# Three rearrangements ahead of the expert stage of a fused decoder layer: one column and the taps in `prepare`, the step tables of the recurrence, and double-buffered sums instead of in-place ones for the shared expert

## What is computed

```python
z = x @ w_in
# group A: GLU, causal depthwise convolution of width 31, LayerNorm, swish
u = z_conv[..., :D_CONV] * sigmoid(z_conv[..., D_CONV:])
c = silu(layer_norm(conv(u_full, conv_w) + conv_b))
# group B: RWKV-7, 8 heads of 64; per token
s = s * w_t + (s @ a_t) b_t^T + v_t k_t^T ;  y_t = s r_t
o_rw = (group_norm(y) * gn_g + gn_b + bonus) * g
x = layer_norm(ALPHA * x + concat(c, o_rw) @ w_out)
# 64 experts, top 8 of each token, hidden width 256, and one shared expert
f = (silu(x @ sh_gate) * (x @ sh_up)) @ sh_down + routed experts
x = layer_norm(ALPHA * x + f)
```

## Time and profile before

| | us |
|---|---|
| median of 3 runs | 1219.98 |
| lowest and highest | 1216.82, 1224.33 |
| the profiled execution | 1224.33 |
| its span, first to last instruction | 1222.5 |
| PE busy in the span | 1093.1 |
| DVE, ACT, POOL busy | 540.6, 278.2, 191.6 |
| mean granted clock of PE, of 2.4 GHz | 0.95 |

### The profile page before, as it was taken

The page is one execution under the profiler, slowest core; times in us unless marked ns, Lnnn a source line. Parts: engine busy times, 40 slices in busy tenths (PEclk is TensorE's granted clock), DMA queues, the critical chain, the costliest instruction groups (busy, mean ns, idle before and its releaser), DMA issues. The chain is left out here.

```text
span 1222.5 us, 33491 instructions
## 1 busy us (share of the span) xinstructions
PE 1093.1 (89%) x14966; PEld 826.4 (68%) x14967; DVE 540.6 (44%) x1216; ACT 278.2 (23%) x583; POOL 191.6 (16%) x202
## 2 busy tenths in 40 slices
PE   6999997888799997999999999999899999999940
PEld 5887886767553584877777777777667676766720
DVE  0778968597475786342222222222222222222105
ACT  2146421122364120111111111111111111111102
POOL 2000100000000011122222212222222122221113
PEclk8999998888799999899999999999999999999975
DMA  7221131400532178999999999999999999999623
GB/s 201 69 53 52 52 88 24 108 7 5 185 105 56 71 276 357 375 342 347 343 341 336 333 327 328 322 321 327 331 331 321 336 338 329 344 330 334 229 34 140
DMA packets 87589, 279.58 MB, mean 229 GB/s; under 512 B 22363, under 2 KB 46948, under 8 KB 62605
## 3 DMA queue, kind: packets, MB, share of 16 engines
q1 hardware_dynamic: 72165, 240.07, 55.0%
q0 software_dynamic: 14336, 34.11, 11.6%
q10 hardware_dynamic: 944, 3.24, 0.7%
HBM read 258.80 MB, written 35.30 MB: 241 GB/s over the span
## 5 line engine op out<-in xcount | busy, mean ns | idle before, releaser
L2141 PE MATMUL pgu<-x_list_t,w_exp 128*64 128x96 f32 x8192 | 361.4, 248 | 23.5 <-DMA w_exp<-in_exp_up_dram 17.2
L2141 PEld LDWEIGHTS pgu<-x_list_t,w_exp 128*64 128x64 f32 x8192 | 344.1, 139 | 32.8 <-DMA w_exp<-in_exp_up_dram 21.6
L2168 PE MATMUL pyl<-w_exp,hid 128*96 128x512 f32 x512 | 230.5, 593 | 3.7 <-issue 2.3
L2195 POOL DMA_INDIRECT scr_f<-y_list,row x64 | 92.1, 1439 | 510.1 <-DVE row L890 159.2
L2156 DVE TENSOR_TENSOR sig<-sig,pgu 128x192 f32<-128x192 f32 x64 | 22.7, 354 | 312.3 <-ACT sig L2149 312.3
L507 PE MATMUL pz<-w_exp 128*128 128x260 f32 x672 | 160.4, 398 | 0.3 <-ACT w_exp L324 0.3
L2168 PEld LDWEIGHTS pyl<-w_exp,hid 128*96 128x96 f32 x512 | 80.1, 166 | 107.4 <-issue 104.1
L507 PEld LDWEIGHTS pz<-w_exp 128*128 128x128 f32 x672 | 131.1, 198 | 24.3 <-issue 3.0
L2186 DVE TENSOR_SCALAR y_list<-pyl,weight 96x512 f32<-96x512 f32 x64 | 47.8, 747 | 188.9 <-PE pyl L2168 149.6
L2149 ACT ACTIVATE sig<-pgu 128x192 f32<-128x192 f32 x64 | 21.2, 331 | 422.7 <-PE pgu L2141 422.7
L162 DVE SCALAR_TENSOR_TENSOR w_exp<-arena,w_exp 128x512 f32<-128x512 f32 x120 | 89.9, 750 | 3.8
(11 more groups left out here) (352 smaller groups left out, 1015.0 us busy)
## 6 DMA issues: line engine op xcount, KB each, us to landing
w_exp<-in_exp_gate_dram SPq DMA_DIRECT2D x64, 1024.0 KB, 38.6
w_exp<-in_exp_up_dram SPq DMA_DIRECT2D x64, 1024.0 KB, 38.8
w_exp<-in_exp_down_dram SPq DMA_DIRECT2D x64, 1024.0 KB, 38.7
w_exp<-in_w_in_dram SPq DMA_DIRECT2D x22, 512.0 KB, 3.9
w_exp<-in_x_prompt_dram SPq DMA_DIRECT2D x8, 512.0 KB, 5.4
w_exp<-in_w_out_dram SPq DMA_DIRECT2D x2, 2048.0 KB, 11.7
scr_x<-arena SPq DMA_DIRECT2D x4, 512.0 KB
scr_f<-arena ACTq DMA_DIRECT2D x4, 512.0 KB, 11.9
```

Source lines behind the costliest of these rows:

```text
L2141: last = nc.tensor.matmul(pgu[64 * half:64 * half + 64, s % 2, (2 * part + j) * CAP:(2 * part + j + 1) * CAP], w[job.slot][:, k, f0:P * ha ...
L2168: last = nc.tensor.matmul(pyl[0:CAP, c, :], hid[:, s % 2, j, :], m.expert_down[job.slot][:, j, c * 512:(c + 1) * 512], start=(j == 0), sto ...
L2195: nc.gpsimd.indirect_dma_start(m.scr_f, bass.IndirectOffsetOnAxis(ap=row[:, job.l:job.l + 1], axis=0), y_list[:, s % 2, :], None, bounds_c ...
```

## The change

Three parts. **A**, in `prepare`: on PE the last GLU column stands directly behind `turn_samples(0)` and the groups of `read_inside` follow one by one between the sample transposes; on DVE the taps are spread among the masks, seven in place of six, and `glu(3)` stands behind all of them but `mask_inside(7)`'s. **B**, in the recurrence: the group norm of tile 0 is inverted, normalised, finished and turned one step earlier, its bonus one step later; `finish_out(1)` moves from behind the loop into step 15, and `turn_out(1)` from the middle of the first mixing product to ahead of `outputs(3)`. **C**, the shared expert: the sum of tile i is written to `f0[:, i % 2]`, two buffers of 1024 columns in `x_area`, and stored from there; `residual(i)` for i of 2 and 3 waits for the store of tile i - 2, ACT's copy of the samples for that of tile 2. The wait for `x1_stored` ahead of `residual(0)` is gone, and so are the waits for the five stores in `experts`; SP waits for them at the end of `recur_and_mix`.

```diff
@@ prepare, PE
                 turn_samples(0)
+                col(cv + 5)
                 read_inside(4)
-                col(cv + 5, lambda: read_inside(5))
                 turn_samples(2)
+                read_inside(5)
+                turn_samples(4)
                 read_inside(6)
-                turn_samples(4)
                 read_inside(7)
@@ prepare, DVE
                 mask_inside(3)
+                taps.take(1)
                 mask_inside(4)
-                taps.take(5)
+                taps.take(2)
                 mask_inside(5)
+                taps.take(2)
                 mask_inside(6)
+                taps.take(2)
                 glu(3)
-                taps.take(1)
                 mask_inside(7)
@@ recur_and_mix, tables
-    INVERT = {10: 0, 13: 1}
-    NORMALISE = {11: 0, 14: 1}
-    FINISH = {12: 0}
-    TURN = {13: 0}
-    SCALE = {9: 0, 13: 1, 14: 2, 15: 3}
+    INVERT = {9: 0, 13: 1}
+    NORMALISE = {10: 0, 14: 1}
+    FINISH = {11: 0, 15: 1}
+    TURN = {12: 0}
+    SCALE = {10: 0, 13: 1, 14: 2, 15: 3}
@@ recur_and_mix, SP, at its end
+                sp.wait_ge(f_stored[0], 16 * 3)
+                sp.wait_ge(f_stored[1], 16 * 2)
@@ recur_and_mix, PE, behind the recurrence
+                turn_out(1)
                 outputs(TM - 1)
                 pe.wait_ge(spent_cleared, 1)
-                mix_part(0, 0, lambda: turn_out(1))
+                mix_part(0, 0)
@@ recur_and_mix, ACT
-                    act.dma_start(m.scr_f[t0:t0 + n, :], x1[0:n, i, :]).then_inc(m.f_stored[i], 16)
+                    act.dma_start(m.scr_f[t0:t0 + n, :], f0[0:n, i % 2, :]).then_inc(f_stored[i % 2], 16)
                 act.wait_ge(f_done, NT)
+                act.wait_ge(f_stored[TM % 2], 16 * (TM // 2))
@@ recur_and_mix, DVE
-                finish_out(1)
...
-                        if i == 0:
-                            dve.wait_ge(x1_stored, 16 * (NT + 2))
+                        if i >= 2:
+                            dve.wait_ge(f_stored[i % 2], 16 * (i // 2))
...
-                        nc.vector.scalar_tensor_tensor(x1[0:n, i, cs], x1[0:n, i, cs], ALPHA, out,
+                        nc.vector.scalar_tensor_tensor(f0[0:n, i % 2, cs], x1[0:n, i, cs], ALPHA, out,
@@ experts, DVE, ACT and POOL, each
-                for i in range(NT):
-                    dve.wait_ge(m.f_stored[i], 16)
```

More of the change, by code:

```diff
@@ L1035, in recur_and_mix @@
         hit_b = halfs[:, 2 * P:2 * P + NT * E].rearrange("p (i e) -> p i e", i=NT)
-        f_sample = m.x_area[0:B, 2 * D:3 * D]
+        f0 = m.x_area[:, 2 * D:4 * D].rearrange("p (b d) -> p b d", b=2)
         cnt = m.cnt
@@ L1110, in recur_and_mix @@
         f_taken = sem("f_taken")
-        m.f_stored = [sem(f"f_stored{i}") for i in range(NT)]
+        f_stored = [sem(f"f_stored{i}") for i in range(2)]
         late = COLS[NCOL - LATE:]
@@ L1782, in _ @@
                 act.wait_ge(f_done, NT)
+                act.wait_ge(f_stored[TM % 2], 16 * (TM // 2))
                 for c in range(4):
-                    last = nc.scalar.copy(f_sample[:, QD * c:QD * (c + 1)], quarter(ph[:, TM % 2, :], c))
+                    last = nc.scalar.copy(f0[0:B, TM % 2, QD * c:QD * (c + 1)], quarter(ph[:, TM % 2, :], c))
                 last.then_inc(sample_moved, 1)
@@ L2062, in residual @@
                         cs = slice(c * 512, (c + 1) * 512)
-                        out = ph[0:n, i % 2, cs] if i < TM else f_sample[:, cs]
-                        nc.vector.scalar_tensor_tensor(x1[0:n, i, cs], x1[0:n, i, cs], ALPHA, out,
+                        out = ph[0:n, i % 2, cs] if i < TM else f0[0:n, i % 2, cs]
+                        nc.vector.scalar_tensor_tensor(f0[0:n, i % 2, cs], x1[0:n, i, cs], ALPHA, out,
                                                        ALU.mult, ALU.add).then_inc(f_taken, 1)
@@ L2269, in _ @@
                 gate_act(act, Job(0))
-                for i in range(NT):
-                    act.wait_ge(m.f_stored[i], 16)
                 for q in range(E):
@@ L2282, in _ @@
                     gather(nc, m, pool, Job(q))
-                for i in range(NT):
-                    pool.wait_ge(m.f_stored[i], 16)
                 for q in range(E):
```

## The result

| | before | after |
|---|---|---|
| median, us | 1219.14 (20 runs) | 1226.61 (20 runs) |
| lowest and highest | 1215.63, 1225.44 | 1221.95, 1231.08 |
| span of the profiled execution | 1222.5 | 1229.0 |
| PE busy | 1093.1 | 1090.0 |

The ratio of the times is 1.0059, 95% interval 1.0044 to 1.0076: +7.2 us, where the forecast was +8.3 and 1228.0. The two profiled spans differ by 6.5 us.

What follows compares the result with a forecast made beforehand. The weight stream was taken as the expert stage's bound, with 35 us of PE slack. +7.3 (C) - 1.3 (A) + 2.3 (B) = +8.3 us: 1224.3 to 1232.6 profiled, 1228 on the 1219.98 median; range 1213 to 1239.

Steps and rivals of the forecast that it cites:

- The bound: Expert stage: the weight stream, 11.4 us a job against PE's 10.1, is the bound; PE has 35 us of slack.
- the dry point: Turn into the expert stage: weights queue empty at 505.1, 5.7 us after the next load's issue; a later start is free until then.
- Part C: Shared expert's residual: store waits start PE 15.6 us later, job 6's up weights land +7.3 us later; bounds 0 and 15.6.
- Store 2: Store of tile 2's sum: issued after residual 2 ends at 484.1, lands 11.9 us later, at 496.0.
- The fifth store: The samples' 32 KB store at the block's end: issued 498.9, landing after 2.1 us in a nearly quiet queue, at 501.
- PE's first row: Start of the expert block: PE begins at about 503.5, 15.6 us later than before.
- The landing into the dry queue: Job 6's up weights: landing 6.9 us after issue in an idle queue, at 522.3 against 514.9.
- Part A: End of prepare: SP's tail comes earlier and DVE's masks end with it; -1.3 us, bounds -2.5 to +1.5.
- Part B: Recurrence: step 9's later add less PE's idle +1.4, moved finish_out(1) and turn_out(1) +0.9; +2.3 us, bounds -6 to +6.
- Nothing absorbed: Turn into the expert stage: the whole 15.6 us delay passes, +16.6 in all, 1237 us; chance 0.22.
- Quick stores: Shared expert: stores take 4.7 us, residuals don't wait, block ends 3 us later; with recurrence at -6, 1213 us; chance 0.12.
- The recurrence at its bad end: Recurrence: both PE idle times return after the wait, +6 there, +12 in all, 1232 us; chance 0.11.

Runs made afterwards that it cites:

- the seven executions: Two of the changed kernel, plus C alone, both holds and both waits of C apart: last up weights 0.3 to 7.9 us later than before.
- C alone: The kernel before with only part C of the change: 1.0037 of before, +4.5 us.
- the changed kernel with the store moved up: Changed kernel, SP's store of the sample states behind one expert's loads instead of two, two more experts' loads before its wait: 1.0028 of before.
- the tables alone: Kernel before with only part B's step tables (tile 0's group norm a step earlier, bonus later); finish_out(1) and turn_out(1) unmoved: 0.9992 of before.
- both holds: Kernel before with six or eighteen unread ACT copies behind the last store issue of recur_and_mix: 0.9988 and 1.0029 of before.
- both waits of C apart: Kernel before with part C but its stores awaited inside experts, not by SP (1.0010); or in-place sums with SP's end-of-block wait replacing those in experts (1.0007).
- B alone: The kernel before with only part B of the change: 1.0003 of before.

## Why the prediction was right, by its steps

**The bound** held. PE waits for up weights at the end and the stream's pitch is 11.4 us a job (649.6 / 57). The sign and the size of the loss come from the lead at the turn. I had put the dry point at 5.7 us behind the next issue and took 8.3 off the delay (15.6 to 7.3), since a load into an idle queue lands sooner; the seven executions put the lead at 6.5. The 5.7 came out near it partly by luck: it read the end of the queue from the landing of job 5's down weights, and behind them the engines still have the `ln2` loads and gathers to carry.

**Part C**, forecast +7.3. The changed kernel's first expert load came 1.04 us earlier than before, so forecasts are to be read 1.04 lower. Residuals 2 and 3 then were due at 481.8 and 486.3 and came at 481.59 and 486.54. From there the steps miss in both directions:
- Store 2 was taken at 11.9 us; ACT's copy was due at 495.0 and came at 491.52. I had taken over the length of stores that stand behind one another in ACT's own queue. In the kernel before, counted in order, the first packet of store 2 starts 6.3 us behind its issue, when those of stores 0 and 1 are through; in the changed kernel nothing stands ahead of stores 2 and 3, their first packets start after 3.9 and 3.5 us, and store 3 landed after 7.8 us.
- The fifth store, 32 KB, was taken at 2.1 us from a quiet queue. From its issue to SP's next block are 5.1 us, against 0.8 where SP doesn't wait for it. Its first data packet starts 3.3 us and its last packet 4.1 us behind its issue, beside the weights of job 5, in flight until 500.8; the row from a quiet queue was the wrong one.
- PE's first row: due 502.5, came 499.64, 12.8 us late (from the first load, 63.69 against 50.92) and not 15.6. (The terms as written add up to 501 + 1.9 = 502.9 for the 503.5 of the forecast, so 0.6 of it is a slip.)
- The landing into the dry queue: 6.9 forecast, 8.7 measured; the first gate/up 7.89 instead of 7.49. A gather of POOL, issued at 514.14, runs beside this load and none ran beside the one of the 6.9. That is a likely reason, and no run tests it.

Up weights of job 6 were due at 521.3 and landed at 520.6. From the first load the loss is 84.65 - 78.0 = 6.7 us there, and 7.9 by the last issue. The runs by time say +4.5 (2.4 to 6.6) for C alone. The term is right in its mechanism, and its size is right in part by luck: a delay too long by 2.8 and a landing too short by 1.8 nearly cancel.

The rule of the Trainium skill (DMA: Bandwidth & Descriptors, "Queues, rings and completion order") by which a DMA engine serves its rings in turn gave about 0 for this term. I read the 10.2 and 11.9 us as speaking against the rule, and that reading was wrong. The packets of the changed kernel from 482.5 to 483.3 us, by queue (q1 is SP's, q10 ACT's, q0 POOL's; number of packets, MB, share of the engines):

```profile
q1 hardware_dynamic: 23, 0.16, 49.8%
q10 hardware_dynamic: 25, 0.10, 33.2%
q0 software_dynamic: 25, 0.06, 20.2%
```

The three queues have equal turns, as the rule says; in the kernel before SP's and ACT's have 111 packets each from 479.0 to 482.5. A store is slow all the same, and the packets show where its time goes. The first packet of tile 0's store starts 3.6 us behind its issue in the kernel before. Its packets are 4 KB and the weights' are 8 KB, and POOL's gathers take a turn too, so that its data takes another 4.6 us; 2.0 us later it is landed, 10.2 in all. The 3 to 4 us ahead of the first packet seem to belong to the traffic: with nothing ahead in ACT's own queue they are 3.3 to 4.0 us beside full engines, and at most 0.8 us for the one store that was issued as the share sank to 0.58 (the 32 KB one of the changed kernel with the store moved up, at 491.69). No run was made to test that.

**Part A**, forecast -1.3. SP's last loads begin at 228.07, against 230.63:

```profile
229.57 0.56 DVE L734 TENSOR_TENSOR w_exp<-pt,w_exp 128x384 f32<-128x384 f32 x1
...
231.04 0.27 DVE L1897 MEMSET x_area<- 128x256 f32 x1 [0.92 <-PEq L268]
...
228.07 1.34 SPq L311 DMA_DIRECT2D arena<-scr_sample  x2
...
229.45 1.02 SPq L312 DMA_DIRECT2D arena<-scr_sample  x1
```

The last mask of DVE (229.57 + 0.56) and SP's last load (229.45 + 1.02) now end within 0.4 us, as forecast. But of the 2.16 us by which the next block starts earlier (231.04 against 233.20), 1.45 were there before A's place (DVE's last solving reduction starts at 211.11 against 212.56). From that reduction to the add of the first step are on average 41.4 us in five executions with A (40.95 to 41.66) and 41.7 in nine without (40.58 to 42.47). A is worth -0.3 us with a scatter of half a microsecond; this term was over-read by one microsecond, inside its bounds.

**Part B**, forecast +2.3. In the changed kernel, against the earlier trace rows:

```profile
307.68 0.20 DVE L1827 RECIPROCAL arena<-arena 128x8 f32<-128x8 f32 x1 [8.78 <-ACT arena L1663]
...
311.63 0.42 DVE L1940 TENSOR_TENSOR x_area<-x_area,pst 128x256 f32<-128x256 f32 x1
...
323.54 0.69 DVE L1839 TENSOR_TENSOR w_exp<-w_exp 128x512 f32<-128x512 f32 x1 [7.38 <-ACT w_exp L1657]
...
325.80 6.35 PE L1407 MATMUL ph<-w_exp,arena 128*128 128x260 f32 x16
...
347.50 0.34 PE L1359 MATMUL pt<-x_area,w_exp 64*32 64x64 f32 x16
```

- The reciprocal of step 9 waits 8.78 us for ACT, and the add comes at 311.63 against 309.12, 3.8 us later measured from step 8's add (297.57 and 298.84). The forecast was 4.1.
- PE's gaps without a releaser, 2.5 and 2.7 us before, are gone or small:

```profile
PE pst L1346 <- issue: 0.5, 1, 0.5
```

  That was taken as a chance. In the six executions with B or its tables PE's matmuls have 0.5 to 3.4 us of such gaps from 300 to 350 us (1.9 on average), in the eight without 4.4 to 7.2 (6.0).
- The packets show what these gaps wait for. All 22 gaps of more than 1 us there, over the fourteen executions, end 1.25 to 1.60 us after a 16 KB transfer of the kind `instruction` has ended. In the kernel before such transfers end at 307.0, 312.85 and 319.05, and PE goes on at 308.46, 314.13 and 320.41. At an instant taken at random between 300 and 350 us such a transfer has ended 1.25 to 1.60 us ago in 6% of the cases. So these gaps are waits for PE's own next instructions. That they shrink with B because PE stands 8 us for DVE meanwhile fits, and no run separates it.
- Not foreseen: `SCALE` moved to step 10, so DVE's third operation of `finish_out(0)` waits 7.38 us for ACT's bonus, at 323.54 above. It does not lengthen the stretch: from step 8's add to step 12's are 37.5 us before and 37.1 after, and on average 35.6 in eight executions without B (33.3 to 37.5) and 35.9 in five with it (34.6 to 37.1). So of the state's 4.1 us next to nothing is left at step 12 (+0.3 between averages whose executions scatter by 4), where I had forecast 2.7 absorbed and 1.4 left.
- From the end of the mean sums (332.15) the outputs begin 15.35 us later, against 14.2: forecast 15.5. From step 12's add to the first mixing row every execution without B has 15.16 or 15.17 us, every one with B 16.21 to 16.23, and the tables alone 14.48; from there to the first expert load B has 85.04 and the others 85.48. So the tail costs 1.05 - 0.44 = +0.6 (forecast +0.9), and the tables cost about nothing or gain a little. In the tail `finish_out(1)` and `turn_out(1)` stand ahead of work that doesn't need them.

B in all is +0.3 + 0.6 = +0.9 by the traces, +0.4 by time (-1.3 to +2.2). The term of +2.3 was mis-sized, inside its bounds: the stall without a releaser shrinks by 4.1 us on average and not by 2.7.

**The rivals.** Nothing absorbed (1237) is refused by both holds and both waits of C apart. Quick stores (1213) is refused by residual 2's wait and the 504 to 512 hole. The recurrence at its bad end (1232) by B alone.

Taken together, the parts were forecast at +7.3, -1.3 and +2.3, and the distances inside the traces put them at +6.7 (7.9 by the last issue), -0.3 and +0.9, together +7.3. That the sum, +8.3, came so near +7.2 owes something to misses of opposite sign.

Left open: for one and the same code the stretch from step 8 to step 12 varies by 4 us between executions. The gaps in it end behind an instruction transfer, but no run here shows why these come later in one execution than in another.

## What to carry to other kernels

Where a stream of loads is the bound, put a number on its lead at each turn of stages (here the landing time of the next load as it stands, less that of the same load in an idle queue, 15.2 - 8.7 us): a wait shorter than the lead is free, several in a row share one lead, and closing an early hole pays only if the queue is not dry again behind it. A store that is waited for right behind its issue costs its landing beside the traffic of that moment, so wait for it in the next stage, behind work that is late anyway. The length of a store is a poor constant: measure from its first packet, and ask what stands ahead of it in its own queue and how many queues take turns. With effects of 1 us and executions that scatter by 10, distances inside the traces between two fixed instructions tell more than medians.

## What the runs showed that I had not expected

- A 32 KB store issued at 494.36 held the block for about 4 us more than no wait at all (5.1 against 0.8 us between the issues).
- From 500 to 504 us, with 15.67 us of idle ahead, PE's granted clock was 0.50 in the changed kernel (1.2 of 2.4 GHz), and in the same stretch of the changed kernel with the store moved up too, in the first of its two rows above. The first gate/up took 7.89 us there, 7.49 in the kernel before behind 5.75 us of idle, and the second one 5.51.
- ACT's stores do not stand behind all of SP's weights: once a store has begun, its packets and theirs go one for one. With nothing ahead of it in ACT's queue, a 512 KB store took 7.7 to 8.2 us without gathers beside it and 8.9 to 10.2 us where gathers ran; behind other stores it took up to 12.2.
- Some stretches are the same to 0.02 us in every execution of the same code (15.16 us from step 12's add to the mixing), others vary by 4 us (step 8 to 12); a single execution is a fair witness for the first kind only.
